# TensorE's operands in another order, by feed-forward: columns from last to first, weights of neighbouring chunks side by side

## The chip, the cores and the metric

The kernel runs on one core of a Trainium2 chip, in one launch. The metric is the device time of that execution in microseconds. An engine's name is given as in the profile: PE is TensorE's matmul part and PEld its weight load, DVE is VectorE, ACT ScalarE, POOL GpSimd, SP SyncE.

## The reference

Two transformer blocks run one after the other on 256 tokens of width 1024, in float32. Only the feed-forward parts matter for this change. Each block has two of them, and each is, up to norms and a residual weight of 0.5:

```python
def swiglu(h, w_gate, w_up, w_down):
    return (jax.nn.silu(h @ w_gate) * (h @ w_up)) @ w_down
```

with h of 256 x 1024, w_gate and w_up of 1024 x 2816 and w_down of 2816 x 1024. Between the two feed-forwards of the first block stand a projection, sparse attention and an mLSTM branch, between those of the second a MoBA attention with a pooling branch and a cross attention to a memory. Two further products per weight element keep the float32 precision, as the next section tells.

## The kernel before

**Three products for one.** Every operand of the large products is held as a rounded part (`_hi`, float32r) and the rest (`_lo`, float32r). A product is the sum of hi x hi, hi x lo and lo x hi, so three matmuls stand where the reference has one. float32r matmuls go through in one pass.

**Units.** All large weights are cut into units of up to 1024 elements per partition, listed once by `Plan` (line 230) in the order in which they are used. `whole` (line 243) cuts a block of `nw` columns into units of UNIT // nw chunks of 128 rows: two chunks for 512 columns, four for 256. Six buffers take the units in turn (STAGES, line 27). SP loads a unit into `stage` (line 386), ACT rounds it into `w_hi` (line 942, `hi_to`), DVE, or POOL for 24 of them, subtracts to get `w_lo` (line 1299, `lo_to`; line 1827, `lop_to`), and PE uses both (line 427, `unit`). A buffer's next load waits for its w_lo, its next w_hi for PE (semaphore `used`). In all three tiles of a buffer a unit lies as [chunk][column]: chunk k's columns are next to each other, chunk k+1 follows `nw` elements later.

**Where the tiles rest.** `Space` (line 107) lays tiles out one after the other in SBUF; where it is given `rest` it moves on until the address modulo 512 bytes is that number. W_REST (line 31) does this for the six weight buffers: 128, 160, 192, 256, 448 and 512, w_hi and w_lo alike. F_REST and H_REST do it for the activations of the four feed-forwards. h_hi and h_lo of the first and third rest at 128.

**Two forms.** In "rows" the activations are the stationary operand (128 x 128) and up to 512 columns of weights move past them; the output has tokens as partitions. In "cols" 128 columns of weights are stationary and 256 tokens of activations move; the output has weight columns as partitions, which is what the next product needs. Both accumulate in PSUM (`pair`), chunk after chunk. The core of `unit`:

```python
            if b.form == "rows":
                for t in ts:
                    o, a_h, a_l = ps[:, t * 512:t * 512 + nw], b.hi[:, k, t * P:(t + 1) * P], b.lo[:, k, t * P:(t + 1) * P]
                    mm(o, a_h, w_h[:, k - k0, :], first, False)
                    mm(o, a_l, w_h[:, k - k0, :], False, False)
                    ins = mm(o, a_h, w_l[:, k - k0, :], False, stop)
            else:
                for g in range(nw // P):
                    o, gs = ps[:, g * S + c0:g * S + c1], slice(g * P, (g + 1) * P)
                    mm(o, w_h[:, k - k0, gs], b.hi[:, k, c0:c1], first and g % 2 == 0 and ts[0] == 0, False)
                    mm(o, w_h[:, k - k0, gs], b.lo[:, k, c0:c1], False, False)
                    ins = mm(o, w_l[:, k - k0, gs], b.hi[:, k, c0:c1], False, stop)
```

**A feed-forward.** It has six blocks of gate and up (FF_BLOCKS, line 227: five of 512 columns, one of 256) and two halves of down. The first block is in rows, and its product is turned by PE afterwards; the other five are in cols. The down halves are in rows again, 22 chunks each. `ffn` at line 249 plans it, `ffn` at lines 486, 970 and after 1333 are its PE, ACT and DVE parts. Behind each block ACT takes the sigmoid out of PSUM (line 983), DVE multiplies twice (lines 1348 and 1357), ACT rounds (line 992) and DVE subtracts (line 1361) to make f_hi and f_lo for the down product. The engines' orders are written out by hand, and each engine runs ahead of PE by up to six units.

The four calls, in order of time, are called first to fourth here: `ffn(0, ...)` to `ffn(3, ...)`. In the trace they show as `pair<-h_hi,w_hi` and the like where weights are stationary (cols, 128x256) and as `pair<-w_hi,h_hi` or `pair<-w_hi,f_hi` where they move (rows, 128x512). The name before the comma is the moving operand.

Of the kernel before, what the change touches and what calls it, by code (L numbers as in the profile page):

```python
# [7 lines left out]
F32 = mybir.dt.float32  # L8
F32R = mybir.dt.float32r
ACT = mybir.ActivationFunctionType  # L10
ALU = mybir.AluOpType
# [6 lines left out]
DC = D // P  # L18
FF = 2816
FC = FF // P  # L20
# [6 lines left out]
STAGES = 6  # L27
# [2 lines left out]
SBUF_START, SBUF_END = 16512, 229368  # L30
W_REST = (128, 160, 192, 256, 448, 512)
F_REST = (448, 128, 0, 32)
H_REST = (None, 448, None, 64)

# [184 lines left out]

Block = namedtuple("Block", "form nw k_first k_last hi lo pair")
Unit = namedtuple("Unit", "block k0 k1 srcs")

IN = {"q": 0, "kv": 512, "iq": 768, "ik_iw": 1280, "mx": 1352, "mv": 1864, "mi_mf": 2376, "mo": 2384, "ga": 2896, "gb": 3920}
# [3 lines left out]
class Plan:  # L230
    def __init__(self, d, m):
# [8 lines left out]
                self.by_pool.add(len(self.units))  # L240
            self.units.append(Unit(block, k0, k1, [(slice(0, P), slice(0, block.nw), kn(w)[:, k0:k1, n0:n0 + block.nw])]))

        def whole(w, K, n0, nw, form, hi, lo, pair, share=False):
            kc = min(K, UNIT // nw)
            b = Block(form, nw, 0, K, hi, lo, pair)
            for k0 in range(0, K, kc):
                add(b, w, n0, k0, min(K, k0 + kc), share)

        def ffn(n, gate, up, down, pairs):
            self.F.append(len(self.units))  # L250
            for n0, nw in FF_BLOCKS:
                form = "rows" if n0 == 0 else "cols"
                whole(gate, DC, n0, nw, form, *m.h_of[(0, 2, 3, 7)[n]], pairs[0])
                whole(up, DC, n0, nw, form, *m.h_of[(0, 2, 3, 7)[n]], pairs[1])
            self.DOWN.append(len(self.units))
            for half in range(2):
                whole(down, FC, 512 * half, 512, "rows", m.f_hi[n], m.f_lo[n], pairs[2 + half])

        def in_halves(w, first, pairs):
            blocks = [Block("rows", 512, 4 * first, DC if first == 0 else 4, m.h_hi, m.h_lo, p) for p in pairs]  # L260
# [68 lines left out]
        for u in range(self.n):  # L329
            n_lo[u in self.by_pool] += 1  # L330
            self.lo_at.append(n_lo[u in self.by_pool])

    def width(self, u):
        b, k0, k1, _ = self.units[u]
# [76 lines left out]
def tensor_program(e, s, m, plan):  # L411
# [8 lines left out]
    def mm(o, l, r, start, stop):  # L420
        return e.matmul(o, l, r, start=start, stop=stop, skip_group_check=True)  # L421
# [5 lines left out]
    def unit(u, ts=(0, 1), half=False):  # L427
        b, k0, k1, _ = plan.units[u]
        ps, nw, slot = m.pair[b.pair], b.nw, u % STAGES
        n = plan.width(u)  # L430
        w_h = m.w_hi[slot][:, 0:n].rearrange("p (k n) -> p k n", n=nw)
        w_l = m.w_lo[slot][:, 0:n].rearrange("p (k n) -> p k n", n=nw)
        if ts[0] == 0:
            if k0 == b.k_first:
                take(b.pair)
            e.wait_ge(*lo_sem(s, plan, u))
        c0, c1 = ts[0] * P, (ts[-1] + 1) * P
        for k in range(k0, k1):
            first, stop = k == b.k_first, k == b.k_last - 1
            if b.form == "rows":  # L440
                for t in ts:
                    o, a_h, a_l = ps[:, t * 512:t * 512 + nw], b.hi[:, k, t * P:(t + 1) * P], b.lo[:, k, t * P:(t + 1) * P]
                    mm(o, a_h, w_h[:, k - k0, :], first, False)
                    mm(o, a_l, w_h[:, k - k0, :], False, False)
                    ins = mm(o, a_h, w_l[:, k - k0, :], False, stop)
            else:
                for g in range(nw // P):
                    o, gs = ps[:, g * S + c0:g * S + c1], slice(g * P, (g + 1) * P)
                    mm(o, w_h[:, k - k0, gs], b.hi[:, k, c0:c1], first and g % 2 == 0 and ts[0] == 0, False)
                    mm(o, w_h[:, k - k0, gs], b.lo[:, k, c0:c1], False, False)  # L450
                    ins = mm(o, w_l[:, k - k0, gs], b.hi[:, k, c0:c1], False, stop)
        if ts[-1] == 1:
            ins.then_inc(s.used, 1)
        elif half:
            ins.then_inc(s.half, 1)
# [476 lines left out]
def scalar_program(e, s, m, plan):  # L932
# [3 lines left out]
    def hi_to(n):  # L936
        for u in range(done[0], min(n, plan.n)):
            w = plan.width(u)
            if u >= STAGES:
                e.wait_ge(s.used, u - STAGES + 1)  # L940
            e.wait_ge(loads[u % STAGES], plan.load_at[u])
            e.copy(m.w_hi[u % STAGES][:, 0:w], m.stage[u % STAGES][:, 0:w]).then_inc(s.hi, 1)  # L942
        done[0] = max(done[0], n)

    def square(src, t, half):
# [344 lines left out]
def vector_program(e, s, m, plan):  # L1290
    done, chained = [0], [0]

    def lo_to(n):
        for u in range(done[0], min(n, plan.n)):
            if u in plan.by_pool:
                continue
            w, slot = plan.width(u), u % STAGES
            e.wait_ge(s.hi, u + 1)
            e.tensor_tensor(m.w_lo[slot][:, 0:w], m.stage[slot][:, 0:w], m.w_hi[slot][:, 0:w].bitcast(F32), ALU.subtract).then_inc(s.lo, 1)  # L1299
        done[0] = max(done[0], n)  # L1300

    def link(ins):
# [507 lines left out]
def gpsimd_program(e, s, m, d, plan):  # L1810
# [10 lines left out]
    def lop_to(n):  # L1821
        for u in range(done[0], n):
            if u not in plan.by_pool:
                continue
            w, slot = plan.width(u), u % STAGES
            e.wait_ge(s.hi, u + 1)
            e.tensor_tensor(m.w_lo[slot][:, 0:w], m.stage[slot][:, 0:w], m.w_hi[slot][:, 0:w].bitcast(F32), ALU.subtract).then_inc(s.lop, 1)  # L1827
        done[0] = max(done[0], n)

    def gain(i, name):  # L1830
# [93 lines left out]
    for g in range(4):  # L1924
        src, dst = m.win[g % 2], m.win[(g + 1) % 2]
# [82 lines left out]
```

## Time and profile before

| | |
|---|---|
| median of 3 runs | 1189.48 us (1189.33 to 1191.98) |
| profiled execution: time, span | 1189.25 us, 1187.4 us |
| PE busy | 1141.6 us, 96% |
| PEld busy | 1031.4 us, 87% |
| DVE, ACT, POOL busy | 700.5, 554.8, 134.0 us |
| mean granted TensorE clock | 0.992 of full |
| first, second, third, fourth feed-forward's cols (matmuls of 256 columns), about | 38 to 140, 437 to 540, 625 to 729, 1017 to 1120 us |

A matmul's busy time in the trace holds the way through the array, so neighbouring matmuls overlap in it (281 ns of busy time for one that is followed 118 ns later by the next). The time that a matmul costs in a stream is therefore read from start to start. A granted clock of ten tenths is 2.4 GHz, one of five tenths 1.2 GHz.

### The profile page before, as it was taken

The page shows a single profiled execution, that of the slowest core. Times are in us where ns is not written, and L with a number is a line of the kernel's source. Part 1 is how long each engine was busy: PE and PEld are TensorE (multiplying, and loading weights), DVE is VectorE, ACT ScalarE, POOL GpSimd, SP SyncE. Part 2 cuts the span into 40 slices and gives each one's busy share as a digit, 9 for nine tenths or more (in the row PEclk, how much of TensorE's full clock was granted, in tenths as well). Part 3 has the DMA queues.
Part 4 walks back from the last instruction along what each step waited for, and adds up shares of the span by engine and source line. Part 5 has one row for each costly group of instructions (what it writes and reads, how often), then busy time and mean ns, then how long its engine had stood idle before and what let it go on. Part 6 is the DMA issues. An engine that isn't in the chain of part 4 may idle for free.

```text
span 1187.4 us, 17705 instructions
## 1 busy us (share of the span) xinstructions
PE 1141.6 (96%) x7518; PEld 1031.4 (87%) x7518; DVE 700.5 (59%) x768; ACT 554.8 (47%) x719; POOL 134.0 (11%) x99
## 2 busy tenths in 40 slices
PE   6999999889899999999999999999999998999998
PEld 5999988877789889998889999888987986999986
DVE  5665644589726665565475575454847537665643
ACT  5544443553743444444354454445746435544441
POOL 1000001444310100000030000014232003000000
PEclk9999999999899999999999999999999999999999
DMA  8756555444444476656566565538344534666550
GB/s 294 226 178 197 187 182 157 161 162 125 133 124 139 141 241 180 181 175 201 173 223 220 160 218 193 192 125 310 125 160 159 196 107 131 217 186 196 179 176 36
DMA packets 112335, 209.71 MB, mean 177 GB/s; under 512 B 8688, under 2 KB 18048, under 8 KB 112128
## 3 DMA queue, kind: packets, MB, share of 16 engines
q1 hardware_dynamic: 109568, 198.60, 52.8%
q0 software_dynamic: 2688, 9.98, 2.5%
q8 instruction: 59, 0.97, 0.4%
q14 instruction: 20, 0.16, 0.0%
HBM read 207.50 MB, written 1.05 MB: 176 GB/s over the span
## 4 chain that ended last, share of the span: by engine, by line
PE 82%; DVE 9%; ACT 3%; POOL 2%; issue 2%; DMA 1%; DVEq 0%; SPq 0%; POOLq 0%; ACTq 0%
PE pair L421 80%; DVE w_lo L1299 3%; PE pair L425 1%; ACT w_hi L942 1%; DVE xr L1325 1%; DMA stage<-in_ffn_w_gate 1%; ACT xr L948 1%; DVE work L1563 1%; POOL stat L1845 1%; DVE work L1546 1%; DVE top L1561 0%; POOL xr L1933 0%; DVE xr L1495 0%; DVE xr L1575 0%; DVE x L1395 0%
## 5 line engine op out<-in xcount | busy, mean ns | idle before, releaser
L1299 DVE TENSOR_TENSOR w_lo<-stage,w_hi 128x1024 fp32r<-128x1024 f32 x351 | 438.2, 1261 | 271.0 <-ACT w_hi L942 270.0
L942 ACT CAST w_hi<-stage 128x1024 fp32r<-128x1024 f32 (+1 forms) x375 | 387.5, 1047 | 336.6 <-PE pair L421 327.0
L421 PE MATMUL pair<-h_hi,w_hi 128*128 128x256 f32 x1504 | 426.4, 284 | 2.9 <-POOL w_lo L1827 1.4
L421 PE MATMUL pair<-h_lo,w_hi 128*128 128x256 f32 x1504 | 423.6, 282 | 0.0
L421 PE MATMUL pair<-h_hi,w_lo 128*128 128x256 f32 x1504 | 423.0, 281 | 0.0
L421 PEld LDWEIGHTS pair<-h_hi,w_hi 128*128 128x128 f32 x1504 | 285.6, 190 | 7.9 <-issue 5.1
L421 PEld LDWEIGHTS pair<-h_hi,w_lo 128*128 128x128 f32 x1504 | 285.5, 190 | 0.0
L421 PEld LDWEIGHTS pair<-h_lo,w_hi 128*128 128x128 f32 x1504 | 285.2, 190 | 0.3
L421 PE MATMUL pair<-w_hi,f_hi 128*128 128x512 f32 x352 | 139.1, 395 | 0.0
L421 PE MATMUL pair<-w_lo,f_hi 128*128 128x512 f32 x352 | 138.7, 394 | 0.0
L421 PE MATMUL pair<-w_hi,f_lo 128*128 128x512 f32 x352 | 138.4, 393 | 0.0
L421 PE MATMUL pair<-w_hi,h_hi 128*128 128x512 f32 (+1 forms) x304 | 121.9, 401 | 9.9 <-DVE w_lo L1299 5.4
L421 PE MATMUL pair<-w_lo,h_hi 128*128 128x512 f32 (+1 forms) x304 | 120.4, 396 | 0.0
L421 PE MATMUL pair<-w_hi,h_lo 128*128 128x512 f32 (+1 forms) x304 | 119.9, 394 | 0.0
L421 PEld LDWEIGHTS pair<-w_hi,h_hi 128*128 128x128 f32 x304 | 58.0, 191 | 26.3 <-issue 6.7
L421 PEld LDWEIGHTS pair<-w_lo,f_hi 128*128 128x128 f32 x352 | 66.1, 188 | 15.6
L421 PEld LDWEIGHTS pair<-w_hi,f_lo 128*128 128x128 f32 x352 | 66.1, 188 | 15.2
L421 PEld LDWEIGHTS pair<-w_hi,f_hi 128*128 128x128 f32 x352 | 66.1, 188 | 15.0
L1827 POOL TENSOR_TENSOR w_lo<-stage,w_hi 128x1024 fp32r<-128x1024 f32 x24 | 64.8, 2703 | 85.5 <-ACT w_hi L942 85.5
L1845 POOL TENSOR_TENSOR stat<-stat,half_pow 128x1 f32<-128x1 f32 x16 | 14.3, 896 | 497.9 <-DVE stat L1316 497.9
L421 PEld LDWEIGHTS pair<-w_lo,h_hi 128*128 128x128 f32 x304 | 57.9, 191 | 12.7
L421 PEld LDWEIGHTS pair<-w_hi,h_lo 128*128 128x128 f32 x304 | 58.0, 191 | 12.0
(254 smaller groups left out, 913.5 us busy)
## 6 DMA issues: line engine op xcount, KB each, us to landing
stage<-in_ffn_w_gate SPq DMA_DIRECT2D x88, 512.0 KB, 4.5
stage<-in_ffn_w_up SPq DMA_DIRECT2D x88, 512.0 KB, 4.4
stage<-in_ffn_w_down SPq DMA_DIRECT2D x88, 512.0 KB, 4.0
stage<-in_w_in SPq DMA_DIRECT2D x52, 512.0 KB, 4.3
stage<-in_w_out SPq DMA_DIRECT2D x16, 512.0 KB, 3.7
stage<-in_xa_wkv SPq DMA_DIRECT2D x16, 512.0 KB, 4.5
stage<-in_xa_wq SPq DMA_DIRECT2D x8, 512.0 KB, 4.3
stage<-in_xa_wo SPq DMA_DIRECT2D x8, 512.0 KB, 3.6
```

The costliest lines, as they stand in the source:

```text
L421: return e.matmul(o, l, r, start=start, stop=stop, skip_group_check=True)
L425: return e.transpose(o, i_, m.ident[0:n, 0:n])
L942: e.copy(m.w_hi[u % STAGES][:, 0:w], m.stage[u % STAGES][:, 0:w]).then_inc(s.hi, 1)
L948: e.activation(m.xr[:, t, cols], src[:, t, cols], ACT.Square, accum_out=m.stat[:, t, half:half + 1]).then_inc(s.sq, 1)
L1299: e.tensor_tensor(m.w_lo[slot][:, 0:w], m.stage[slot][:, 0:w], m.w_hi[slot][:, 0:w].bitcast(F32), ALU.subtract).then_inc(s.lo, 1)
L1325: e.scalar_tensor_tensor(m.xr[:, t, cols], src[:, t, cols], r, m.pre_gain[:, cols], ALU.mult, ALU.mult).then_inc(s.xr, 1)
L1546: ins = e.scalar_tensor_tensor(m.work[t][:], src, iw, m.work[t][:], ALU.mult, ALU.add)
L1563: link(e.match_replace(m.work[t][:], m.top[:], m.work[t][:], PICKED))
L1827: e.tensor_tensor(m.w_lo[slot][:, 0:w], m.stage[slot][:, 0:w], m.w_hi[slot][:, 0:w].bitcast(F32), ALU.subtract).then_inc(s.lop, 1)
L1845: e.tensor_tensor(m.stat[:, t, 3:4], m.stat[:, t, 2:3], m.half_pow[:, 0:1], ALU.pow).then_inc(s.rt, 1)
```

## The change

A field `walk` is added to the planned blocks, and a table WALK gives it for the four feed-forwards. With "back" the moving operand and the output are both taken from the last column to the first, so each result lands where it did. With "pairs" a unit of the cols form lies in w_hi and w_lo as [column][chunk] instead of [chunk][column], which puts the same column of two chunks (four in the block of 256 columns) side by side; the stationary operand is then read with a step of two (four) elements. ACT's and DVE's (POOL's) instructions write it so through another view of the same tiles; the load into `stage` stays as it is. All other products (projections, attention, mLSTM) keep their order.

| call | cols | rows |
|---|---|---|
| first | back | back |
| second | back and pairs | as before |
| third | pairs | back |
| fourth | as before | as before |

On every engine the instructions, their order, their sizes and their waits are the same before and after. What differs are the access patterns: 72 of ACT's 375 casts and 72 of DVE's 351 subtractions have an output of [2 chunks, step 1][512 columns, step 2] or [4, step 1][256, step 4] where it was one run of 1024, and DVE's second source, w_hi, likewise. No unit that POOL handles is in the paired layout.

```diff
--- before.py
+++ after.py
@@ -30,6 +30,9 @@
 SBUF_START, SBUF_END = 16512, 229368
 W_REST = (128, 160, 192, 256, 448, 512)
 F_REST = (448, 128, 0, 32)
+
+
+WALK = ({"cols": "back", "rows": "back"}, {"cols": "back pairs", "rows": ""}, {"cols": "pairs", "rows": "back"}, {"cols": "", "rows": ""})
 H_REST = (None, 448, None, 64)
 
 
@@ -220,7 +223,7 @@
 
 
 
-Block = namedtuple("Block", "form nw k_first k_last hi lo pair")
+Block = namedtuple("Block", "form nw k_first k_last hi lo pair walk", defaults=("",))
 Unit = namedtuple("Unit", "block k0 k1 srcs")
 
 IN = {"q": 0, "kv": 512, "iq": 768, "ik_iw": 1280, "mx": 1352, "mv": 1864, "mi_mf": 2376, "mo": 2384, "ga": 2896, "gb": 3920}
@@ -240,9 +243,9 @@
                 self.by_pool.add(len(self.units))
             self.units.append(Unit(block, k0, k1, [(slice(0, P), slice(0, block.nw), kn(w)[:, k0:k1, n0:n0 + block.nw])]))
 
-        def whole(w, K, n0, nw, form, hi, lo, pair, share=False):
+        def whole(w, K, n0, nw, form, hi, lo, pair, share=False, walk=""):
             kc = min(K, UNIT // nw)
-            b = Block(form, nw, 0, K, hi, lo, pair)
+            b = Block(form, nw, 0, K, hi, lo, pair, walk)
             for k0 in range(0, K, kc):
                 add(b, w, n0, k0, min(K, k0 + kc), share)
 
@@ -250,11 +253,11 @@
             self.F.append(len(self.units))
             for n0, nw in FF_BLOCKS:
                 form = "rows" if n0 == 0 else "cols"
-                whole(gate, DC, n0, nw, form, *m.h_of[(0, 2, 3, 7)[n]], pairs[0])
-                whole(up, DC, n0, nw, form, *m.h_of[(0, 2, 3, 7)[n]], pairs[1])
+                whole(gate, DC, n0, nw, form, *m.h_of[(0, 2, 3, 7)[n]], pairs[0], False, WALK[n][form])
+                whole(up, DC, n0, nw, form, *m.h_of[(0, 2, 3, 7)[n]], pairs[1], False, WALK[n][form])
             self.DOWN.append(len(self.units))
             for half in range(2):
-                whole(down, FC, 512 * half, 512, "rows", m.f_hi[n], m.f_lo[n], pairs[2 + half])
+                whole(down, FC, 512 * half, 512, "rows", m.f_hi[n], m.f_lo[n], pairs[2 + half], False, WALK[n]["rows"])
 
         def in_halves(w, first, pairs):
             blocks = [Block("rows", 512, 4 * first, DC if first == 0 else 4, m.h_hi, m.h_lo, p) for p in pairs]
@@ -330,6 +333,13 @@
             n_lo[u in self.by_pool] += 1
             self.lo_at.append(n_lo[u in self.by_pool])
 
+    def laid(self, u, tile):
+
+        b, n = self.units[u].block, self.width(u)
+        if b.form == "cols" and "pairs" in b.walk:
+            return tile[:, 0:n].rearrange("p (n k) -> p k n", n=b.nw)
+        return tile[:, 0:n].rearrange("p (k n) -> p k n", n=b.nw)
+
     def width(self, u):
         b, k0, k1, _ = self.units[u]
         return (k1 - k0) * b.nw
@@ -430,25 +440,38 @@
         n = plan.width(u)
         w_h = m.w_hi[slot][:, 0:n].rearrange("p (k n) -> p k n", n=nw)
         w_l = m.w_lo[slot][:, 0:n].rearrange("p (k n) -> p k n", n=nw)
+        pairs_h = m.w_hi[slot][:, 0:n].rearrange("p (n k) -> p n k", n=nw)
+        pairs_l = m.w_lo[slot][:, 0:n].rearrange("p (n k) -> p n k", n=nw)
         if ts[0] == 0:
             if k0 == b.k_first:
                 take(b.pair)
             e.wait_ge(*lo_sem(s, plan, u))
         c0, c1 = ts[0] * P, (ts[-1] + 1) * P
+        back = slice(None, None, -1)
         for k in range(k0, k1):
             first, stop = k == b.k_first, k == b.k_last - 1
             if b.form == "rows":
                 for t in ts:
                     o, a_h, a_l = ps[:, t * 512:t * 512 + nw], b.hi[:, k, t * P:(t + 1) * P], b.lo[:, k, t * P:(t + 1) * P]
-                    mm(o, a_h, w_h[:, k - k0, :], first, False)
-                    mm(o, a_l, w_h[:, k - k0, :], False, False)
-                    ins = mm(o, a_h, w_l[:, k - k0, :], False, stop)
+                    r_h, r_l = w_h[:, k - k0, :], w_l[:, k - k0, :]
+                    if b.walk == "back":
+                        o, r_h, r_l = o[:, back], r_h[:, back], r_l[:, back]
+                    mm(o, a_h, r_h, first, False)
+                    mm(o, a_l, r_h, False, False)
+                    ins = mm(o, a_h, r_l, False, stop)
             else:
                 for g in range(nw // P):
                     o, gs = ps[:, g * S + c0:g * S + c1], slice(g * P, (g + 1) * P)
-                    mm(o, w_h[:, k - k0, gs], b.hi[:, k, c0:c1], first and g % 2 == 0 and ts[0] == 0, False)
-                    mm(o, w_h[:, k - k0, gs], b.lo[:, k, c0:c1], False, False)
-                    ins = mm(o, w_l[:, k - k0, gs], b.hi[:, k, c0:c1], False, stop)
+                    r_h, r_l = b.hi[:, k, c0:c1], b.lo[:, k, c0:c1]
+                    if b.walk in ("back", "back pairs"):
+                        o, r_h, r_l = o[:, back], r_h[:, back], r_l[:, back]
+                    if b.walk in ("pairs", "back pairs"):
+                        l_h, l_l = pairs_h[:, gs, k - k0], pairs_l[:, gs, k - k0]
+                    else:
+                        l_h, l_l = w_h[:, k - k0, gs], w_l[:, k - k0, gs]
+                    mm(o, l_h, r_h, first and g % 2 == 0 and ts[0] == 0, False)
+                    mm(o, l_h, r_l, False, False)
+                    ins = mm(o, l_l, r_h, False, stop)
         if ts[-1] == 1:
             ins.then_inc(s.used, 1)
         elif half:
@@ -939,7 +962,7 @@
             if u >= STAGES:
                 e.wait_ge(s.used, u - STAGES + 1)
             e.wait_ge(loads[u % STAGES], plan.load_at[u])
-            e.copy(m.w_hi[u % STAGES][:, 0:w], m.stage[u % STAGES][:, 0:w]).then_inc(s.hi, 1)
+            e.copy(plan.laid(u, m.w_hi[u % STAGES]), m.stage[u % STAGES][:, 0:w].rearrange("p (k n) -> p k n", n=plan.units[u].block.nw)).then_inc(s.hi, 1)
         done[0] = max(done[0], n)
 
     def square(src, t, half):
@@ -1296,7 +1319,8 @@
                 continue
             w, slot = plan.width(u), u % STAGES
             e.wait_ge(s.hi, u + 1)
-            e.tensor_tensor(m.w_lo[slot][:, 0:w], m.stage[slot][:, 0:w], m.w_hi[slot][:, 0:w].bitcast(F32), ALU.subtract).then_inc(s.lo, 1)
+            src = m.stage[slot][:, 0:w].rearrange("p (k n) -> p k n", n=plan.units[u].block.nw)
+            e.tensor_tensor(plan.laid(u, m.w_lo[slot]), src, plan.laid(u, m.w_hi[slot]).bitcast(F32), ALU.subtract).then_inc(s.lo, 1)
         done[0] = max(done[0], n)
 
     def link(ins):
...
```

The hunk left out changes `lop_to` of POOL as the one above it changes `lo_to`.

## Rows read from the trace of the kernel before

**Rows 1.** The page: span, busy time of the engines, granted clock in 40 slices.
```profile
span 1187.4 us, 17705 instructions
...
PE 1141.6 (96%) x7518; PEld 1031.4 (87%) x7518; DVE 700.5 (59%) x768; ACT 554.8 (47%) x719; POOL 134.0 (11%) x99
...
PEclk9999999999899999999999999999999999999999
```

**Rows 2.** The page: the chain that ended last, by engine and by line.
```profile
PE 82%; DVE 9%; ACT 3%; POOL 2%; issue 2%; DMA 1%; DVEq 0%; SPq 0%; POOLq 0%; ACTq 0%
PE pair L421 80%; DVE w_lo L1299 3%; PE pair L425 1%; ACT w_hi L942 1%; DVE xr L1325 1%; DMA stage<-in_ffn_w_gate 1%; ACT xr L948 1%; DVE work L1563 1%; POOL stat L1845 1%; DVE work L1546 1%; DVE top L1561 0%; POOL xr L1933 0%; DVE xr L1495 0%; DVE xr L1575 0%; DVE x L1395 0%
```

**Rows 3.** Who waited for whom: total us, times, longest us.
```profile
PE pair L421 <- DVE w_lo L1299: 7.0, 7, 3.0
```

**Rows 4.** PE in eight stretches: from:to, length, busy (matmuls), clock, DMA, GB/s.
```profile
52.00:137.00 85.00, 85.00 (x725) 1.00 0.59 180
141.00:198.00 57.00, 57.00 (x249) 1.00 0.55 167
449.00:536.00 87.00, 87.00 (x737) 1.00 0.59 179
541.00:598.00 57.00, 57.00 (x248) 1.00 0.54 169
640.00:678.00 38.00, 38.00 (x325) 1.00 0.56 167
730.00:788.00 58.00, 58.00 (x252) 1.00 0.50 166
1030.00:1112.00 82.00, 82.00 (x697) 1.00 0.60 186
1121.00:1181.00 60.00, 60.00 (x258) 1.00 0.36 115
```

**Rows 5.** Timeline of PE: start, us, what. Units in the fifth buffer, first call.
```profile
61.22 0.28 PE L421 MATMUL pair<-h_hi,w_hi 128*128 128x256 f32 x1
61.34 0.28 PE L421 MATMUL pair<-h_lo,w_hi 128*128 128x256 f32 x1
...
63.83 0.28 PE L421 MATMUL pair<-h_hi,w_lo 128*128 128x256 f32 x1
...
78.18 0.28 PE L421 MATMUL pair<-h_hi,w_hi 128*128 128x256 f32 x1
...
80.79 0.28 PE L421 MATMUL pair<-h_hi,w_lo 128*128 128x256 f32 x1
```

**Rows 6.** Timeline of PE and PEld, a unit in the first buffer, first call.
```profile
84.46 0.28 PE L421 MATMUL pair<-h_hi,w_hi 128*128 128x256 f32 x1
84.46 0.19 PEld L421 LDWEIGHTS pair<-h_lo,w_hi 128*128 128x128 f32 x1
84.58 0.28 PE L421 MATMUL pair<-h_lo,w_hi 128*128 128x256 f32 x1
...
86.14 0.28 PE L421 MATMUL pair<-h_hi,w_lo 128*128 128x256 f32 x1
```

**Rows 7.** Groups of PEld by form: busy us, mean ns, idle before.
```profile
L421 PEld LDWEIGHTS pair<-h_hi,w_hi 128*128 128x128 f32 x1504 | 285.6, 190 | 7.9 <-issue 5.1 <-DVE h_lo L1333 1.2 <-DVE w_lo L1299 0.8
...
L421 PEld LDWEIGHTS pair<-pt,v 128*64 128x64 f32 x32 | 2.0, 136 | 1.2 <-issue 0.5
```

**Rows 8.** Groups by form, 449 to 536 us; the POOL row is of the whole span.
```profile
L1299 DVE TENSOR_TENSOR w_lo<-stage,w_hi 128x1024 fp32r<-128x1024 f32 x30 | 36.2, 1222 | 21.1 <-ACT w_hi L942 21.1
L942 ACT CAST w_hi<-stage 128x1024 fp32r<-128x1024 f32 x31 | 32.0, 1047 | 26.3 <-PE pair L421 26.3
...
L1827 POOL TENSOR_TENSOR w_lo<-stage,w_hi 128x1024 fp32r<-128x1024 f32 x24 | 64.8, 2703 | 85.5 <-ACT w_hi L942 85.5
```

**Rows 9.** All engines, second call's cols: length, busy of PE, PEld, DVE, ACT, POOL.
```profile
449.00:536.00 87.00, 87.00 (x737) 87.00 (x736) 52.08 (x44) 40.73 (x41) 0.00 (x0) 1.00 0.59 179
```

**Rows 10.** Timeline of PE: sixteen plain float32 matmuls of the cross attention, merged.
```profile
929.05 3.61 PE L421 MATMUL pair<-xk,xq 128*128 128x256 f32 x16
...
L421 PE MATMUL pair<-xk,xq 128*128 128x256 f32 x32 | 7.2, 379 | 0.0
```

More of the change, by code:

```diff
@@ L1826, in lop_to @@
             e.wait_ge(s.hi, u + 1)
-            e.tensor_tensor(m.w_lo[slot][:, 0:w], m.stage[slot][:, 0:w], m.w_hi[slot][:, 0:w].bitcast(F32), ALU.subtract).then_inc(s.lop, 1)
+            src = m.stage[slot][:, 0:w].rearrange("p (k n) -> p k n", n=plan.units[u].block.nw)
+            e.tensor_tensor(plan.laid(u, m.w_lo[slot]), src, plan.laid(u, m.w_hi[slot]).bitcast(F32), ALU.subtract).then_inc(s.lop, 1)
         done[0] = max(done[0], n)
```

## The prediction

> **What bounds the kernel now.** I read the page's busy shares and its chain of waits first, then TensorE stretch by stretch, then single matmuls, and last what ACT and DVE do beside them. The span is 1187.4 us and the matmul engine is busy for 1141.6 us of it, at a granted clock of ten tenths nearly everywhere, which is the 2.4 GHz level [rows 1]. The chain that ended last is 82% PE, and one matmul line alone has 80% [rows 2]. In all PE waits some 7.0 us for halves of weights that DVE makes [rows 3]. So the time is the number of matmuls times the distance from one start to the next, and a change of operand order counts only through that distance.
>
> That distance I take from stretches in which PE never rests [rows 4], length over count, the count less three (256 columns) or two (512 columns) for matmuls that only reach in. "cols" matmuls, 256 columns wide: 85.00/722 = 117.7 ns in the first feed-forward, 87.00/734 = 118.5 in the second, 38.00/322 = 118.0 in the third, 82.00/694 = 118.2 in the fourth. "rows" matmuls, 512 wide: 57.00/247 = 230.8, 57.00/246 = 231.7, 58.00/250 = 232.0, 60.00/256 = 234.4. The four calls differ by 1 to 2%.
>
> Inside a call the distance is not even. Twenty-three steps from 61.22 to 63.83 us take 113.5 ns each; fourteen from 84.46 to 86.14 take 120.0 [rows 5, 6]. Same shapes, same clock, same tiles' names: what differs is the weight slot, and each of the six slots rests at another address (W_REST). The good distance is back six units later, 23 steps from 78.18 to 80.79 us at 113.5 ns [rows 5]. So the reads of TensorE get in each other's way by some nanoseconds, depending on how the addresses of the moving operand and of the next weights lie to each other. This is what the change can touch: between 113.5 and 120.0 ns the trace shows what an order can give or take while the read rate itself is kept.
>
> **The change, part by part.** One feed-forward has 864 matmuls of 256 columns (18 column groups x 8 chunks x 2 matrices x 3 products) and 360 of 512 (96 in the first block of gate and up, 264 in down). Columns go from last to first in both forms of the first call, in cols of the second and in rows of the third: 1728 narrow and 720 wide matmuls, 1728 x 118 ns + 720 x 231 ns = 370 us of PE time. Weights lie side by side in cols of the second and third: 1728 matmuls, 204 us. No instruction is added or removed, none moves, and no wait is new.
>
> (1) Other phases between the reads. Where a slot now has a good or a bad distance it will have another. Lower bound: all 2592 narrow matmuls of three calls go at the best slot's distance, 2592 x (113.5 - 118.0) = -11.7 us, and the 720 wide ones save the same 4.5 ns each, -3.2 us. Upper bound: 2592 x (120.0 - 118.0) = +5.2 us, and 720 x (234.4 - 231.5) = +2.1 us by the slowest call. I take 0: against a stream that runs the other way, or twice as fast, the reads pass through all distances, and the average over the slots is what stands there now.
>
> (2) Weight loads with a step of two elements. A load of 128 columns takes 190 ns and one of 64 columns 136 ns [rows 7], so 54/64 = 0.84 ns a column, 108 ns for 128: it is hidden behind the matmul before it, with about 10 ns to spare. A load that walks over 1,016 bytes for its 128 values may meet the moving stream twice as often as one over 508. What meets now is worth 118.0 - 113.5 = 4.5 ns. So 0 to +4.5 ns for 1728 matmuls, 0 to +7.8 us. The value lies nearer to the lower end, since values are still taken one in 0.84 ns: I take a quarter, +2 us. In the last block (256 columns wide, four chunks a unit) the step is four elements; this is 192 of the 1728.
> The Trainium skill (SBUF — State Buffer, in the note on cachelines of its section on the port swizzle) says that four fp32 values share a line, and that two hits on a line are enough for the full rate. By it the step of two costs nothing and only the step of four could; no row here shows either.
>
> (3) The casts of ACT and the subtractions of DVE, 72 of each, write with that step, and DVE reads one source so. The rows have 1047 ns for ACT's and 1222 ns for DVE's [rows 8], all unstepped. In 87.00 us of the second feed-forward DVE is busy for 52.08 and ACT for 40.73 [rows 9]; there are 30 subtractions. DVE's could take (87.00 - 52.08)/30 = 1.16 us longer each, 2.38 us in all, before DVE passes PE; ACT's have 1.5 us to spare. The nearest row for a slow one is GpSimd's same operation, 2703 ns [rows 8]: 52.08 + 30 x 1.48 = 96.5 us in place of 87.00, +9.5, and +11 for the 102 us of cols of a call; two calls, +22 us. The lower bound is 0: all sources and outputs keep their counts. I take 0, since 1.95 times the present duration would be needed. If the cover goes, the next late thing is w_lo, and PE waits at its line 436.
>
> Sum: 1189.25 us (the profiled execution: span 1187.4 and 1.85 around it) + 0 + 2 + 0 = 1191.3; the median of the runs is 0.2 us above that execution, so **1191.5 us**. A measurement of this kernel tells about 0.3%, 3.6 us, from no change.
>
> **The rivals.**
> A. Reads that run against each other meet only briefly, and the excess over the best slot goes. For it: the gap of 113.5 to 120.0 ns is real and depends on addresses alone. Against: two of three calls would have to gain in all slots, and the second and third also get the stepped loads. Price: up to -15 us, 1174 to 1186.
> B. Descending columns do not keep the rate, in the read or in the PSUM write. Then a matmul goes at one column in two cycles. What that looks like is in the trace: plain fp32 products of xk and xq, 256 wide, go at (3.61 - 0.38)/15 = 215 ns a step at the same clock [rows 10]. Price: 1728 x (215 - 118) + 720 x (430 - 231) = +168 + 143 = +311 us, 1500 us. It decides as soon as pairs of neighbouring elements are only merged upwards. For it: at 118 ns for 256 columns TensorE is so near to what its reads give that an address matters. Against: nothing in the trace descends.
> The Trainium skill (Advanced Engine Details and Errata, PSUM Cachelines) says that any access that is not contiguous slows matmuls markedly; whether a step of -1 counts as that it doesn't say. If it does, this rival is what it means.
> C. The stepped loads meet the moving stream twice as often, term (2) at its upper end, alone or with (1) at its: +8 to +15 us, 1197 to 1205. This is the one that ends slower by a mechanism that the trace already shows at work.
> D. DVE becomes the bound in cols of the second and third feed-forward: from 2.38 us a subtraction, +3 to +22 us more, up to 1214.
> E. A weight load with a step takes twice as long, 216 ns, and sets the pace: 1728 x (216 - 118) = +169 us, 1361 us. It decides as soon as a load exceeds 118 ns, 10% more than now.
> That the change does not do what it says is excluded for the sums: output and moving operand are turned together, and the weights' layout is turned at both ends.
>
> **How the numbers follow.** No measurable change 0.30, the likeliest single case, within 3.6 us of 1189.5. A 0.25. C 0.22, D 0.05. B 0.14, E 0.04. So faster 0.25, same 0.30, slower 0.45. The range leaves out B and E, 0.18 together, and holds the rest: low 1189.5 - 15 = 1174, high 1189.5 + 7 + 8 + 22 = 1227. The likeliest case's own range is 1186 to 1193.
>
> **What would show it.** Start-to-start distances in the same stretches: cols of calls one to three at 117 to 119 ns, rows at 230 to 233, the fourth call as before (118.2, 234.4). If A holds, narrow matmuls at 114 to 116 in the first call. If B holds, 215 and 430 wherever columns run back, and the third call's cols (pairs, not back) near 118. If C or E holds, the third call's cols above 120 or at 216 with its rows unchanged. If D holds, w_lo rows above 2.38 us and waits of PE for w_lo of several us. The forecast is wrong if one of the first three calls is off by over 2 us where the fourth is not.

## The result, and the profile after

The changed kernel takes 1217.22 us (median of 4 runs, 1215.20 to 1218.01), the kernel before on the same chip 1190.73 (4 runs, 1189.33 to 1192.53): ratio 1.0219, 95% interval 1.0206 to 1.0232. It is **slower by 26.5 us**. The forecast was 1191.5, no measurable change; the time is inside the stated range, but far outside the likeliest case.

The page of the changed kernel, its span, the engines' busy time, the granted clock in slices and the chain that ended last (to be read against [rows 1, 2]):

```profile
span 1213.4 us, 17705 instructions
...
PE 1168.1 (96%) x7518; PEld 1056.1 (87%) x7518; DVE 707.4 (58%) x768; ACT 570.4 (47%) x719; POOL 133.4 (11%) x99
...
PEclk9999999989999999999999999999999999999999
...
PE 83%; DVE 9%; POOL 3%; ACT 2%; issue 2%; DMA 1%; DVEq 0%; SPq 0%; POOLq 0%; ACTq 0%
```

The span grew by 26.0 us and PE's busy time by 26.5. DVE and ACT grew too, by 6.9 and 15.6 us, but neither got longer in the chain. The clock is the same. The waits of PE for w_lo, in the changed kernel (total us, times, longest), against 7.0 us in [rows 3]:

```profile
PE pair L431 <- DVE w_lo L1323: 6.6, 7, 3.1
```

So PE waits no more than before: the 26 us lie in the distance between its matmuls. PE in ten stretches of the changed kernel, the same columns as in [rows 4]; the fourth and the seventh row are the last blocks (256 columns, step of four) of the second and third call:

```profile
52.00:137.00 85.00, 85.00 (x719) 1.00 0.58 178
142.00:199.00 57.00, 57.00 (x246) 1.00 0.55 166
450.00:529.00 79.00, 79.00 (x666) 1.00 0.56 177
531.00:552.00 21.00, 21.00 (x91) 1.00 0.41 134
554.00:611.00 57.00, 57.00 (x248) 1.00 0.47 157
650.00:688.00 38.00, 38.00 (x319) 1.00 0.59 180
734.00:755.00 21.00, 21.00 (x91) 1.00 0.37 133
757.00:815.00 58.00, 58.00 (x250) 1.00 0.47 155
1056.00:1138.00 82.00, 82.00 (x697) 1.00 0.58 185
1147.00:1207.00 60.00, 60.00 (x258) 1.00 0.33 116
```

A stretch of 21 us with 91 matmuls stands beside one of 38 us with 319. Both are full (busy equals length), both at the full clock, and the busy share shows no difference between them; the count does. Worked out from the matmuls' starts, the distances are, in ns:

| part | matmuls | before | after | us |
|---|---|---|---|---|
| first call, cols (back) | 864 | 118.0 | 118.7 | +0.6 |
| first call, rows (back) | 360 | 230.6 | 233.5 | +1.0 |
| second call, cols of 512 (back, step 2) | 768 | 118.5 | 119.0 | +0.4 |
| second call, last block (back, **step 4**) | 96 | 118.5 | 234.5 | **+11.1** |
| second call, rows (unchanged) | 360 | 231.4 | 231.5 | 0 |
| third call, cols of 512 (step 2) | 768 | 118.0 | 120.7 | +2.0 |
| third call, last block (**step 4**) | 96 | 118.0 | 233.5 | **+11.1** |
| third call, rows (back) | 360 | 231.5 | 233.9 | +0.9 |
| fourth call (unchanged) | 1224 | 118.2, 233.5 | 118.2, 233.5 | 0 |

The sum is +27.1 us where the spans differ by 26.0. The two last blocks, 192 of 7518 matmuls, hold 22.2 us of it. The switch can be seen to the matmul. PE and PEld in the second call of the changed kernel, timeline with start and duration in us:

```profile
530.21 0.20 PEld L431 LDWEIGHTS pair<-h_hi,w_lo 128*128 128x128 f32 x1
530.32 0.28 PE L431 MATMUL pair<-h_hi,w_lo 128*128 128x256 f32 x1
530.33 0.31 PEld L431 LDWEIGHTS pair<-h_hi,w_hi 128*128 128x128 f32 x1
530.44 0.40 PE L431 MATMUL pair<-h_hi,w_hi 128*128 128x256 f32 x1
530.54 0.33 PEld L431 LDWEIGHTS pair<-h_lo,w_hi 128*128 128x128 f32 x1
530.67 0.40 PE L431 MATMUL pair<-h_lo,w_hi 128*128 128x256 f32 x1
530.77 0.33 PEld L431 LDWEIGHTS pair<-h_hi,w_lo 128*128 128x128 f32 x1
530.91 0.40 PE L431 MATMUL pair<-h_hi,w_lo 128*128 128x256 f32 x1
```

At 530.33 the load goes from 0.20 us to 0.31 and then 0.33, and the starts from 0.12 us apart to 0.23 or 0.24. The load's group in 531 to 552 us, changed kernel (busy us, mean ns), where [rows 7] have 190 ns:

```profile
L431 PEld LDWEIGHTS pair<-h_hi,w_lo 128*128 128x128 f32 x31 | 10.2, 331 | 0.0
```

DVE and ACT slowed in the same blocks: groups of 450 to 514 us (step 2) and of 516.5 to 529 us (step 4, made ahead for the last block; the ACT group holds one plain cast of 1.06 us beside four of 2.09 to 2.27), changed kernel, against 1047 and 1222 ns in [rows 8]:

```profile
L965 ACT CAST w_hi<-stage 128x1024 fp32r<-128x1024 f32 x23 | 26.8, 1185 | 18.1 <-PE pair L431 18.1
L1323 DVE TENSOR_TENSOR w_lo<-stage,w_hi 128x1024 fp32r<-128x1024 f32 x22 | 26.6, 1224 | 15.8 <-ACT w_hi L965 15.8
...
L965 ACT CAST w_hi<-stage 128x1024 fp32r<-128x1024 f32 x5 | 9.5, 1954 | 2.9 <-PE pair L431 2.9
L1323 DVE TENSOR_TENSOR w_lo<-stage,w_hi 128x1024 fp32r<-128x1024 f32 x4 | 8.6, 2188 | 3.6 <-ACT w_hi L965 3.6
```

So two things have a step of four, the loads of PE and the writes that fill the tiles, and the trace alone does not tell which one costs. The experiments do. They compare with the kernel before on the same chip; distances are from starts as above. A time without a number of runs is that of a single run.

### The profile page after: what moved, and what is told of

Same layout as the page of the kernel before. It is cut to its first block, busy times and chain, and to the rows that moved or that the text cites. A ratio compares the mean times of both kernels' runs of the same rounds, so it can differ in the third digit from the quotient of the medians.

```text
span 1213.4 us, 17705 instructions
## 1 busy us (share of the span) xinstructions
PE 1168.1 (96%) x7518; PEld 1056.1 (87%) x7518; DVE 707.4 (58%) x768; ACT 570.4 (47%) x719; POOL 133.4 (11%) x99
## 4 chain that ended last, share of the span: by engine, by line
PE 83%; DVE 9%; POOL 3%; ACT 2%; issue 2%; DMA 1%; DVEq 0%; SPq 0%; POOLq 0%; ACTq 0%
PE pair L431 81%; DVE w_lo L1323 3%; PE pair L435 1%; DVE xr L1349 1%; ACT w_hi L965 1%; POOL stat L1870 1%; DMA stage<-in_ffn_w_gate 1%; DVE work L1587 1%; DVE work L1570 0%; ACT xr L971 0%; DVE top L1585 0%; POOL xr L1958 0%; DVE xr L1519 0%; DVE xr L1599 0%; DVE x L1419 0%
## 5 line engine op out<-in xcount | busy, mean ns | idle before, releaser
L1323 DVE TENSOR_TENSOR w_lo<-stage,w_hi 128x1024 fp32r<-128x1024 f32 x351 | 445.2, 1282 | 283.2 <-ACT w_hi L965 282.3
L965 ACT CAST w_hi<-stage 128x1024 fp32r<-128x1024 f32 (+1 forms) x375 | 403.1, 1090 | 336.9 <-PE pair L431 328.5
L431 PE MATMUL pair<-h_hi,w_hi 128*128 128x256 f32 x1504 | 435.5, 290 | 3.0 <-POOL w_lo L1852 1.5
L431 PE MATMUL pair<-h_hi,w_lo 128*128 128x256 f32 x1504 | 431.7, 287 | 0.0
L431 PE MATMUL pair<-h_lo,w_hi 128*128 128x256 f32 x1504 | 431.6, 287 | 0.0
L431 PEld LDWEIGHTS pair<-h_hi,w_hi 128*128 128x128 f32 x1504 | 297.4, 198 | 8.2 <-issue 5.5
L431 PEld LDWEIGHTS pair<-h_lo,w_hi 128*128 128x128 f32 x1504 | 297.4, 198 | 0.3
L431 PEld LDWEIGHTS pair<-h_hi,w_lo 128*128 128x128 f32 x1504 | 296.9, 197 | 0.0
L431 PE MATMUL pair<-w_lo,h_hi 128*128 128x512 f32 (+1 forms) x304 | 120.1, 395 | 0.0
L431 PEld LDWEIGHTS pair<-w_hi,f_hi 128*128 128x128 f32 x352 | 66.2, 188 | 15.6
```

Of the source, the lines that this page charges most:

```text
L965: e.copy(plan.laid(u, m.w_hi[u % STAGES]), m.stage[u % STAGES][:, 0:w].rearrange("p (k n) -> p k n", n=plan.units[u].block.nw)).then_inc(s ...
L1323: e.tensor_tensor(plan.laid(u, m.w_lo[slot]), src, plan.laid(u, m.w_hi[slot]).bitcast(F32), ALU.subtract).then_inc(s.lo, 1)
```

## The experiments

### e1: all of the change but the step of four

```diff
+                walk = WALK[n][form]
+                if nw == 256:
+                    walk = {"back pairs": "back", "pairs": "twos"}.get(walk, walk)
```

> The changed kernel, but no weight load with a step of four: in the last gate and up block (256 columns) the second call has plain weights (columns still run back), the third call has its four chunks as two times two, a step of two. Theory L (a load with a step of four elements takes some 233 ns and sets the pace of the 96 matmuls of such a block): both blocks fall from 233.4 ns a matmul to 118 to 121, and the time by 2 x 96 x 114 ns = 21.9 us, to about 1195 us. Rival K (it is the four chunks of that block or the reversed columns, not the step): the block of one of the two calls stays at 233 ns, the time falls by 11 us at most.

Measured: 1194.99 us (5 runs) against 1190.12, ratio 1.0048 (1.0028 to 1.0068). The last blocks of the second and third call in e1, 11 us each:

```profile
527.50:538.50 11.00, 11.00 (x95) 1.00 0.53 169
719.00:730.00 11.00, 11.00 (x94) 1.00 0.49 170
```

They are at 118.5 and 120.2 ns, where the changed kernel needs 21 us for 91 matmuls. What is left, +4.9 us, is what the table's other rows give (0.6 + 1.0 + 0.4 + 2.0 + 0.9). The step of four in two blocks is 1217.22 - 1194.99 = 22 us.

### e2: writes alone, reads alone

In the last block only: the second call writes w_hi and w_lo with the step of four and reads them plainly, the third writes plainly and reads with it.

```diff
-        if b.form == "cols" and "pairs" in b.walk:
+        if b.walk == "write":
...
-                    if b.walk in ("pairs", "back pairs"):
+                    if b.walk == "read":
```

> The kernel before, with one half of the step of four in one block each (the last gate and up block; the numbers computed there are not the reference's, since one half of the rearrangement is left out). Second call: ACT and DVE write with the step, TensorE reads in one run. Third call: they write in one run, TensorE's weight loads have the step. Theory L: second call's block at 118 ns a matmul, third's at 233 ns, 1189.5 + 11 = 1200.5 us. Rival W (ACT's and DVE's stepped writes, 2.1 to 2.2 us each, slow TensorE down, by port or by lateness): second call's block at 233 ns, third's at 118, the same total.

Measured: 1203.6 us, 3 us above the expected total; 11.1 us of the 13.5 over the kernel before lie in the third call's block, and the rest is within the spread of single runs (1187.2 to 1192.0 us for the kernel before). The two blocks, PE, in e2:

```profile
530.00:541.00 11.00, 11.00 (x95) 1.00 0.52 194
719.30:740.30 21.00, 21.00 (x95) 1.00 0.34 113
```

Writing: 118.5 ns a matmul, as before, though the casts and subtractions among it are slow. Reading: 233.4 ns. **The whole cost is in the stationary operand's read**; the writes, twice as long, stay hidden, since only the 4 units of that block have them and ACT and DVE are ahead.

### e3: which step costs what

Loads of another step in the last block of each call, from plain tiles: 3, 4, 8 and 2 elements in the first to fourth.

```diff
+                    if b.walk.startswith("step"):
+                        st = int(b.walk.split()[1])
...
+                            at = (k - k0) * 2 + g
+                            l_h, l_l = (t[:, at:at + 127 * st + 1:st] for t in (m.w_hi[slot], m.w_lo[slot]))
```

> The kernel before, where in the last gate and up block the weight loads alone have a step of 3, 4, 8 and 2 elements in the first to fourth call (which weights a matmul gets is changed there, so the output is not the reference's; all else as before). Theory L with a cost that rises where neighbouring values no longer share 16 bytes by two: step 2 at 120 ns, step 3 between 120 and 233, steps 4 and 8 both at 233. Rival (cost by the distance covered): step 3 at about 180 and step 8 far above 233.

Measured: 1220.84 us. The last blocks of the four calls in e3:

```profile
129.00:145.00 16.00, 16.00 (x93) 1.00 0.45 137
537.50:558.50 21.00, 21.00 (x91) 1.00 0.33 111
738.00:759.00 21.00, 21.00 (x89) 1.00 0.30 103
1140.50:1151.50 11.00, 11.00 (x94) 1.00 0.52 166
```

| step of the load | 1 | 2 | 3 | 4 | 8 |
|---|---|---|---|---|---|
| ns from start to start | 118 | 120.4 | 176.1 | 233.7 | 241.6 |

No cliff at four and no growth with the width walked: 3 adds half of what 4 adds (58 and 116 ns), and 8 little more than 4. The times of 3 and 4 are as 3 to 4, which is the number of different groups of four neighbouring elements that 128 values touch: 96 and 128, at 1.83 ns a group both times (176.1/96, 233.7/128). A step of two touches 64 groups, 117 ns by the same rate, just under the 118 ns that cover it; a plain load, 32 groups, is set by its 0.84 ns a value. That is an inference from four points, with 8 three per cent above it.
The Trainium skill (SBUF — State Buffer, the note on cachelines in its section on the port swizzle) has such lines of 16 bytes, four fp32 values, and wants two hits on each. The step of four has one hit a line and costs, the step of two has two and nearly doesn't: the trace agrees at these two points. That three, with 1.33 hits a line, stands between them is not in that note.

### e5: the same loads under wider matmuls

If a stepped load stops the stream, it adds its time under any matmul; if it only takes long, a matmul of 512 columns (231 ns) hides it. In the rows form of the first, second and third call activations are read with a step of 2, 4 and 8.

```diff
+                    if b.walk.startswith("step"):
+                        st = int(b.walk.split()[1])
+                        at = min(k * S, FC * S - 128 * 8) // 8 * 8 + k % 2 + 2 * t
+                        a_h, a_l = (flat(q[:])[:, at:at + 127 * st + 1:st] for q in (b.hi, b.lo))
```

> The kernel before, where in the down products (matmuls of 512 columns) the stationary activations are loaded with a step of 2, 4 and 8 in the first to third call and without in the fourth (it multiplies other activations than the reference does there). Theory L says that a load costs nothing as long as the matmul before it is longer: step 2 at 231, steps 4 and 8 at 233 to 236 ns, total at most 2 us over the kernel before. Rival (a stepped load takes bandwidth from the moving operand itself, whatever hides it): steps 4 and 8 at 345 ns or more, 264 x 2 x 115 ns = +60 us.

Measured: 1194.35 us. The rows stretches of the four calls in e5, to be read against the even rows of [rows 4]:

```profile
141.00:198.00 57.00, 57.00 (x247) 1.00 0.54 168
542.00:599.00 57.00, 57.00 (x242) 1.00 0.50 168
733.00:793.00 60.00, 60.00 (x246) 1.00 0.48 159
1126.00:1186.00 60.00, 60.00 (x259) 1.00 0.34 116
```

232.2, 237.6 and 245.6 ns, and 233.5 without a step. The 115 ns that the step of four costs under 256 columns are 6 ns under 512 (231.4 to 237.6), and 14 for eight (231.5 to 245.6): **the load runs beside the matmul and sets the pace only where it is longer**. By e3 these two loads take 233.7 and 241.6 ns, 2 and 10 ns more than the matmul that covers them; the other 4 ns of each are not explained. So the expected 236 ns and 2 us were too low: the three calls give (1.6 + 6.2 + 14.1) x 264 matmuls = 5.8 us by their distances, and the total is 4.2 us above the kernel before.

### e6 and e7: one walk at a time, in all calls

```diff
+WALK = ({"cols": "back", "rows": "back"},) * 4
```

> The kernel before with all columns of all four feed-forwards from last to first, in cols and rows, and no paired weights. By the stretches of the changed kernel (cols back 118.7 ns a matmul for 118.0 before, rows back 233.5 and 233.9 for 230.6 and 231.5): cols within 1 ns of before in every call, rows at 233 to 234 in every call, the fourth (233.5 before) unchanged; 3 x 360 x 2.5 ns + 4 x 864 x 0.6 ns = +5 us, 1195 us. Rival (running back is free, and the rows' 2.5 ns come from something else in the changed kernel): 1190 us, rows as before.

```diff
+WALK = ({"cols": "pairs", "rows": ""},) * 4
...
+                walk = WALK[n][form] if nw == 512 else ""
```

> The kernel before with weights side by side (a step of two) in the four blocks of 512 columns of every call's cols, and the block of 256 columns plain. By the third call of the changed kernel (120.5 ns for 118.0): all four calls at 120 to 121 ns in those blocks, 4 x 768 x 2.4 ns = +7 us, 1197 us. Rival (the 2.5 ns are the third call's own, by its addresses): some call at 118 or less, the total within 3 us of before.

Measured: e6 1194.31 us (7 runs) against 1190.31, ratio 1.0039 (1.0021 to 1.0057). e7 1196.24 (5 runs), ratio 1.0053 (1.0034 to 1.0071). The first call of e6, cols and rows, and then, in a fence of its own, cols of the first and second call of e7:

```profile
52.00:137.00 85.00, 85.00 (x719) 1.00 0.58 178
142.00:199.00 57.00, 57.00 (x246) 1.00 0.56 167
```

```profile
50.00:128.00 78.00, 78.00 (x651) 1.00 0.59 179
455.00:532.00 77.00, 77.00 (x644) 1.00 0.61 181
```

Back gives 118.4 to 119.3 ns in cols and 233.4 to 234.0 in rows, the step of two 120.1 to 120.6, in every call. So walking back keeps the full rate and costs a little all the same (+0.7 ns in narrow, +2 ns in wide matmuls), and a load with a step of two costs about 2.3 ns under a stream that runs forward. Under one that runs back it costs less: the changed kernel's second call has both and is at 119.0 ns, where e6 has 118.4 for back alone.

Within a call the units of e6 still differ by their buffer, 117.7 to 120.0 ns; what is missing from them is the 113.5 ns of [rows 5].

### e8 and e9: good addresses, forward and back

The prediction took from [rows 5, 6] that a plain order gains where the addresses are good: there w_hi rests at 448 and the moving h at 128 (modulo 512): the moving operand's address less the stationary one's is 192 modulo 512. e8 is the kernel before with that distance in the cols of all four calls; in its down rows the weights at 448 move and f rests at 192, which gives 256. e9 is e8 with all walks of the feed-forwards back.

```diff
-W_REST = (128, 160, 192, 256, 448, 512)
-F_REST = (448, 128, 0, 32)
+W_REST = (448,) * 6
+F_REST = (192,) * 4
...
-H_REST = (None, 448, None, 64)
+H_REST = (None, 128, None, 128)
```

> The kernel before with other resting places alone: all six weight buffers at 448 modulo 512, f_hi and f_lo at 192, the h tiles of the second and fourth call at 128 as those of the first and third are. Theory P (the 4 to 6 ns over the best slot's distance are set by where the moving operand and the next weights lie to each other modulo 512, and the slot at 448 against h at 128 is the good one): every cols unit of the feed-forwards at 113.5 to 114.5 ns, 4 x 864 x 4.4 ns = -15 us, with the mixers' cols some -20 us, 1170 us. Rival (the good slot is good because its neighbours rest elsewhere, or by chance): cols stay at 117 to 120 ns in all slots, 1190 us or above.

> The resting places of the run beside it, with all columns of the four feed-forwards from last to first. Theory P and: running back spoils the distance. Then cols are at 117 to 120 ns again and this is 12 to 20 us slower than the run beside it. Rival (running back keeps the distance): 114 ns, within 4 us of the run beside it.

Measured: **e8 1172.78 us** (6 runs) against 1190.31, ratio 0.9851 (0.9822 to 0.9879), the fastest of all. e9 1187.83 (10 runs), ratio 0.9987 (0.9973 to 1.0002). Cols of the first call, of the third in two parts and of the fourth, and rows of the fourth, in e8:

```profile
50.00:136.00 86.00, 86.00 (x762) 1.00 0.61 187
...
625.00:673.00 48.00, 48.00 (x426) 1.00 0.57 166
683.00:715.00 32.00, 32.00 (x274) 1.00 0.57 182
...
1013.00:1103.00 90.00, 90.00 (x766) 1.00 0.59 182
1105.00:1163.00 58.00, 58.00 (x257) 1.00 0.37 120
```

113.3 ns in all buffers of the first and second call, and 226.7 in the down rows of all four. From 674.8 us on in the third call and in the whole fourth it is 117.8, with equal addresses, so the expected 113.5 to 114.5 ns came in two and a half of four calls. e9, first call, cols and rows:

```profile
50.00:136.00 86.00, 86.00 (x732) 1.00 0.60 180
142.00:198.00 56.00, 56.00 (x241) 1.00 0.56 166
```

117.9 and 233.3: a stream that runs back does not see the good distance. At both sets of addresses (e6, e9) it is near to the average of forward streams at mixed addresses.

### e4: a step in the moving operand

The last block of the calls reads its moving operand with a step of 2, 8 and 4, the fourth back.

```diff
+                    if b.walk.startswith("move"):
+                        st = int(b.walk.split()[1])
+                        at = k if st == 8 else 1024 * (k // 4) + k % 4
+                        r_h, r_l = (flat(t[:])[:, at:at + 255 * st + 1:st] for t in (b.hi, b.lo))
```

> The kernel before, where in the last gate and up block (256 columns, 96 matmuls a call) the moving operand is read with a step of 2, 8 and 4 elements in the first, second and third call (other activations than the reference's are multiplied there) and from last to first in the fourth. It measures what a step costs on the other operand. If the same rule holds as for weight loads (step 2 keeps its rate, step 4 and 8 have one element a 16 byte line), but at twice the rate of elements: step 2 at 213 ns a matmul or more, since two elements a cycle no longer come from 8 bytes; steps 4 and 8 at 427 ns or more; the fourth call's block at 118 to 120. Rival (the moving operand tolerates steps within a line): step 2 at 118 to 121 ns.

Measured: 1221.95 us. The four last blocks in e4:

```profile
130.00:150.00 20.00, 20.00 (x89) 1.00 0.38 112
541.00:561.00 20.00, 20.00 (x94) 1.00 0.36 116
740.00:761.00 21.00, 21.00 (x91) 1.00 0.33 107
1142.00:1152.50 10.50, 10.50 (x91) 1.00 0.50 167
```

228.0 ns for a step of 2, 217.6 for 8, 233.1 for 4, 119.2 for back. Of the steps tried all but one and minus one about halve the rate, two already, and a wider one costs no more than that; that four and eight would take 427 ns or more was wrong. The Trainium skill's two hits on a line (SBUF — State Buffer, same note) would let the step of two pass for free; for the moving operand this run shows otherwise. That the moving operand's elements come two a cycle out of 8 bytes, as the expectation supposes, no run shows. An output with a step was not tried.

### e10: is it that distance, or any near it

```diff
+W_REST = (448,) * 6
+F_REST = (128, 192, 256, 192)
...
+H_REST = (None, 96, None, 160)
```

> As the run with other resting places, but h of the second call 32 bytes lower (96) and of the fourth 32 bytes higher (160), and f at 128, 192, 256 and 192. There the first call and half of the third ran at 113.3 ns a matmul and the fourth call at 117.8 throughout, with equal addresses modulo 512. If the distance has a tolerance of 32 bytes, second and fourth call are at 113.3 or 117.8 again, by how each burst of matmuls begins, and rows at 226.7 with every f; total 1165 to 1180 us. Rival (exactly 192 bytes are needed): second and fourth call at 118 to 120 in changing patterns, total 1180 us or above.

Measured: 1178.13 us (4 runs) against 1188.94, ratio 0.9919 (0.989 to 0.9948). Cols of the second call, then of the first, of the third in two parts and of the fourth, in e10:

```profile
444.00:534.00 90.00, 90.00 (x761) 1.00 0.60 182
...
52.00:137.00 85.00, 85.00 (x748) 1.00 0.62 192
630.00:678.00 48.00, 48.00 (x426) 1.00 0.55 165
684.00:716.00 32.00, 32.00 (x284) 1.00 0.61 196
1020.00:1105.00 85.00, 85.00 (x720) 1.00 0.59 177
```

h at 96 gives 118.8 ns, at 160 118.4, at 128 (first and third call) 113.5 to 113.7: 32 bytes to either side lose the gain. Rows: stationary f at 128 228.9 ns, at 192 226.7 and 226.8, at 256 233.3. So the rows' best distance of those tried is 256 bytes, and at 192, the good one in cols, they are slowest. The total fell in the range of the expected tolerance, but the distances in cols are the rival's; 226.7 with every f was wrong too. The second part of the third call runs at 113.7 here and at 118 in e8, with the same addresses there. The kernel before has the 192 bytes once more, in its second call (h at 448, the buffer at 256): of the six units in that buffer one goes at 113.5 ns, five at 117.8. So the address is needed and doesn't suffice; what sets the rhythm at a stretch's start **stays open**.

## Why the prediction was wrong, and where it was right

**The step that failed is term (2)**, at "the step is four elements; this is 192 of the 1728". It said what was different about these loads and then priced them like the rest, a quarter of a meeting each, some 0.2 us for all of them. They cost 22.2 us. The right reading was at hand: a load had 108 ns by [rows 7] and 118 ns of cover, so only 10% more was needed for it to set the pace, as rival E says; and 192 x (233.5 - 118) = 22 us is E confined to the last blocks. E took all 1728 loads or none, at 0.04, and the forecast had no case for a few of them. The sentence behind it had even set the two steps apart: by the Trainium skill (SBUF — State Buffer, same note) the step of four alone could cost. It named the loads that did, and no rival came of it. With E's own price for those 192 (216 ns), the sum would have been 1191.5 + 19 = 1210 us.

**That 1217 us lies in the range is luck.** The mechanism that the forecast used for slower loads ends at 1205 (rival C); the range goes on to 1227 only because the 22 us of rival D are added, and D did not come. By its own sign, one of the first three calls off by over 2 us and the fourth not, the forecast fails: the second and the third call are slower by 11.5 and 14.0 us.

**Term (2), step of two.** +2 us forecast; 2.0 us in the third call and at most 0.4 in the second. Right in size, and e7 gives 2.3 ns in all calls where the stream runs forward. The reason given, reads that meet more often, isn't shown. A load that has just lost its cover is not the reason: 64 groups at 1.83 ns are 117 ns, and in the second call of the changed kernel three of the six buffers go at 117.8 ns with such loads. Rival C's range for it alone, up to 4.5 ns, was too high.

**Term (1).** 0 forecast; +2.9 us measured (0.6 + 1.0 + 0.4 + 0.9), within its bounds of -15 and +7. The reason given for 0, that a stream running the other way passes all distances and so keeps the average, isn't borne out: e6's units run back and still differ by buffer, 117.7 to 120.0 ns. Back loses the good slots, which before had 113.5 ns, and rows go to 233.5 in each call; why the average moved so little isn't shown.

**Term (3).** 0 forecast and right, by e2. DVE's subtractions stay at 1224 ns with a step of two, and reach 2188 with four, under the 2.38 us at which the working set the limit; ACT's go from 1047 to 1185 and 2,086 to 2,269 ns. Only 4 units of each of the two calls are that slow, and PE waits no longer than before. The estimate by the Trainium skill (Vector Engine (DVE) Microarchitecture Reference, 5.2) was 2.6 us, by a step of 24 words; at four words the row has 2.19. Its price in the prediction was also summed wrongly: 72 subtractions, each 0.2 us over 2.38, are some 15 us, not 8. Rival D did not come.

**Term (4).** Right: e6 walks back everywhere at 119 and 234 ns, nowhere 215 or 430. Rival B, the dearest at +311 us and a chance of 0.14, is out for steps of minus one. Its rate exists for other steps: e4 has it for two, four and eight in the moving operand. The Trainium skill (Advanced Engine Details and Errata, PSUM Cachelines) calls what is not contiguous slow; a step of minus one isn't meant by that, as these rows show.

**Rival A** fell: the narrow matmuls of the first call went to 118.7, not 114 to 116. The gain that it pointed at exists, 17.5 us in e8 with rows and mixers in it, but walking back gives it away (e9 against e8: 15 us).

**The sum** with the measured terms: 1190.7 + 2.9 + 2.0 + 22.2 = 1217.8 us, measured 1217.2.

## What to carry to other kernels

When operands are walked in another order, price each step that occurs, with its own count, and ask of each load how much cover it has: here the plain load had 10 ns in 118, and 2.5% of the matmuls made 84% of the loss. In these runs a step in the stationary operand is nearly hidden up to two elements under 256 moving columns (+2.3 ns) and up to four under 512 (+6 ns); in the moving operand only one and minus one of the five steps tried are fast. If a kernel is bound by the distance between matmuls, look at that distance buffer by buffer: a spread of 113.5 to 120.0 ns over equal matmuls is worth more than an order, and part of it was had here by moving tiles (e8, -1.5%).

## What was not expected of the hardware

- The best distances are 113.3 ns for 256 and 226.7 ns for 512 columns, 17/16 of a cycle of 2.4 GHz for each column, in every buffer of the first and second call once the addresses fit (e8).
- The fit is sharp: tiles moved by 32 bytes lose all of it in cols (e10), it is another distance in rows (256 bytes, not 192), and at these addresses it holds for streams that run forward only (e9).
- With equal addresses there are two lasting rhythms, 113.3 and 117.8 ns; the first may turn into the second behind an interruption of 0.9 us by eight other matmuls and stay there (e8, third call at 674.8 us), or come back behind the next one (e10, third call at 686.7 us). The cause is open.
- A step of three in a load costs 176 ns, between two and four, so a rule with one threshold does not describe it (e3).
